# Attention scores of two heads in one alternating block, with the gate's matmul on 64 rows

## The reference

```python
log_f = jax.nn.log_sigmoid((proj[..., 3 * D:] + b_f).astype(jnp.float32))
cum = jnp.cumsum(log_f, axis=1).transpose(0, 2, 1)
s = jnp.einsum('bqhd,bkhd->bhqk', q, k) * HEAD_DIM ** -0.5
s = s + cum[:, :, :, None] - cum[:, :, None, :]
s = jnp.where(mask, s, -jnp.inf)
pr = jax.nn.softmax(s, axis=-1)
out = jnp.einsum('bhqk,bkhd->bqhd', pr, v)
```

## Time and profile before

| | |
|---|---|
| Time, median of 3 runs | 1496.22 us (1495.9 to 1497.05) |
| Span of the profiled execution | 1498.1 us (its own time outside the span is not shown) |
| TensorE busy | 1415.4 us, 94% of the span |
| TensorE weight loads | 1242.7 us, 83% |
| VectorE busy | 1002.6 us, 67% |
| ScalarE busy | 807.3 us, 54% |
| GpSimd busy | 423.5 us, 28% |
| Granted TensorE clock, mean | 0.972 of full speed |
| First score matmul of layers 0, 1, 2, 3 | 91.99, 470.9, 813.52, 1185.3 us |

### The profile page before, as it was taken

How to read it: one execution, slowest core, us unless ns; L and a number is a source line. 1 busy time by engine, 2 the same in 40 slices (tenths; PEclk the granted TensorE clock), 3 DMA queues, 4 the chain that set the end, 5 groups by cost and what they waited for, 6 DMA issues and landing times. The chain is left out here.

```text
span 1498.1 us, 24861 instructions
## 1 busy us (share of the span) xinstructions
PE 1415.4 (94%) x8532; PEld 1242.7 (83%) x8532; DVE 1002.6 (67%) x1577; ACT 807.3 (54%) x1397; POOL 423.5 (28%) x459
## 2 busy tenths in 40 slices
PE   5989899999998989999987989999999899999998
PEld 4767799988776779998876879998878677999986
DVE  4757677764766867775566867776476665777644
ACT  4536466653544746664354656665355454666533
POOL 3521023320165603331027102332006311233200
PEclk9989999999999999999998799999999899999999
DMA  7422265564553345566452136566454322555651
GB/s 281 158 89 82 99 203 178 187 199 145 187 195 129 113 140 173 178 184 198 165 186 88 43 106 191 181 184 197 153 189 155 126 71 85 184 181 184 197 180 57
DMA packets 63927, 232.99 MB, mean 156 GB/s; under 512 B 7184, under 2 KB 7312, under 8 KB 63856
## 3 DMA queue, kind: packets, MB, share of 16 engines
q1 hardware_dynamic: 61056, 221.87, 45.1%
q0 software_dynamic: 2800, 10.18, 2.2%
HBM read 230.97 MB, written 1.05 MB: 155 GB/s over the span
## 5 line engine op out<-in xcount | busy, mean ns | idle before, releaser
L607 DVE TENSOR_TENSOR w_lo<-w_raw,w_hi 128x1024 fp32r<-128x1024 f32 x418 | 561.8, 1383 | 123.2 <-ACT w_hi L379 122.4
L379 ACT ACTIVATE w_hi<-w_raw 128x1024 fp32r<-128x1024 f32 x418 | 420.0, 1052 | 152.7 <-PE bank L1073 112.3
L1049 PE MATMUL bank<-hT_hi,w_hi 128*128 128x256 f32 x1408 | 400.9, 285 | 4.3 <-DVE hT_lo L661 4.3
L1050 PE MATMUL bank<-hT_lo,w_hi 128*128 128x256 f32 x1408 | 400.4, 284 | 0.0
L1051 PE MATMUL bank<-hT_hi,w_lo 128*128 128x256 f32 x1408 | 400.4, 284 | 0.0
L1049 PEld LDWEIGHTS bank<-hT_hi,w_hi 128*128 128x128 f32 x1408 | 271.2, 193 | 5.1 <-issue 5.1
L1050 PEld LDWEIGHTS bank<-hT_lo,w_hi 128*128 128x128 f32 x1408 | 271.3, 193 | 0.0
L1051 PEld LDWEIGHTS bank<-hT_hi,w_lo 128*128 128x128 f32 x1408 | 271.1, 193 | 0.0
L1035 POOL TENSOR_TENSOR gate_c<-gate_c,up_c 128x256 f32<-128x256 f32 x88 | 105.2, 1195 | 293.1 <-ACT gate_c L582 293.1
L887 DVE SCALAR_TENSOR_TENSOR gate_c<-bank,conv_sb,gate_c 128x255 f32<-128x255 f32 (+1 forms) x176 | 84.1, 478 | 120.5 <-ACT up_c L578 120.5
L1049 PE MATMUL bank<-w_hi,hT_hi 128*128 128x512 f32 (+1 forms) x336 | 136.0, 405 | 12.5 <-DVE w_lo L607 6.8
(11 more groups left out here) (136 smaller groups left out, 2289.8 us busy)
## 6 DMA issues: line engine op xcount, KB each, us to landing
w_raw<-weights SPq DMA_DIRECT2D x418, 512.0 KB, 3.9
gain<-gains POOLq DMA_DIRECT2D x11, 512.0 KB, 4.8
rel<-rel_in POOLq DMA_DIRECT2D x4, 512.0 KB, 6.4
x<-x_in SPq DMA_DIRECT2D x2, 512.0 KB, 6.2
p_raw<-p_in POOLq DMA_DIRECT2D x4, 256.0 KB, 5.1
out<-x SPq DMA_DIRECT2D x2, 512.0 KB, 2.6
gain<-gains SPq DMA_DIRECT2D x1, 512.0 KB, 6.4
consts<-consts_in POOLq DMA_DIRECT2D x1, 488.0 KB, 6.3
```

Source lines behind the costliest of these rows:

```text
L379: nc.scalar.activation(w_hi[:, slot, q * HALF:(q + 1) * HALF], w_raw[:, raw, :], ACT.Copy).then_inc(hi_ready, 1)
L607: nc.vector.tensor_tensor(w_lo[:, slot, cols], w_raw[:, half(q)[0], :], w_hi[:, slot, cols].bitcast(F32), ALU.subtract).then_inc(lo_ready, 1)
L1049: nc.tensor.matmul(out_ap, l_hi, r_hi, start=start, stop=False, skip_group_check=True)
L1050: nc.tensor.matmul(out_ap, l_hi, r_lo, start=False, stop=False, skip_group_check=True)
```

## The change

`scores(h)` becomes `score_pair(pair)`. Its matmuls alternate between the two heads of the pair: high x high of the even head (rows 0 to 63), high x high of the odd one (rows 64 to 127), then high x low of both, low x high of both. In FoX the gate's matmul uses the 64 rows of its head's half in place of all 128; for that `cum` and `sel` get a second copy, from row 64 on, by one more ScalarE and one more VectorE instruction in each FoX layer, and by constants. `score_pair(0)` stands ahead of the loop, and the others in odd steps: in step h, the scores of heads h + 1 and h + 2, which wait for the masks of heads up to h.

```diff
                         act.wait_ge(cum_zero, 1)
+                        nc.scalar.activation(cum[HD:HD + HEADS, :], fz[:], ACT.Copy)
                         nc.scalar.activation(cum[0:HEADS, :], fz[:], ACT.Copy).then_inc(cum_hi_ready, 1)
...
                         dve.wait_ge(cum_hi_ready, k + 1)
-                        nc.vector.tensor_tensor(cum[CUM_LO:CUM_LO + HEADS, :], fz[:], cum[0:HEADS, :].bitcast(F32),
-                                                ALU.subtract).then_inc(cum_ready, 1)
+                        for r in (HD + CUM_LO, CUM_LO):
+                            ins = nc.vector.tensor_tensor(cum[r:r + HEADS, :], fz[:], cum[0:HEADS, :].bitcast(F32), ALU.subtract)
+                        ins.then_inc(cum_ready, 1)
...
-                def scores(h):
-
-                    g = HEADS * L + h
-                    if h >= 2:
-                        pe.wait_ge(s_min, 2 * (g - 1))
-                    if m == SWA and h == 8:
+                def score_pair(pair):
+
+                    g = HEADS * L + 2 * pair
+                    if pair:
+                        pe.wait_ge(s_min, 2 * g)
+                    if m == SWA and pair == 4:
                         pe.wait_ge(qkT_ready, item0 + 6)
-                    r = slice((h % 2) * HD, (h % 2) * HD + HD)
-                    kp = h // 8 if m == SWA else h // 2
+                    kp = pair // 4 if m == SWA else pair
+                    halves = [slice(0, HD), slice(HD, P)]
                     for qb in range(2):
-                        dst = aux[h % 2][:, qb * SEQ:(qb + 1) * SEQ]
+                        cols = slice(qb * SEQ, (qb + 1) * SEQ)
                         ts = slice(qb * P, (qb + 1) * P)
-                        last = three(dst, qT_hi[r, h // 2, ts], qT_lo[r, h // 2, ts], kT_hi[r, kp, :], kT_lo[r, kp, :],
-                                     True, m != FOX)
+                        for left, right in ((qT_hi, kT_hi), (qT_hi, kT_lo), (qT_lo, kT_hi)):
+                            for e, r in enumerate(halves):
+                                last = nc.tensor.matmul(aux[e][:, cols], left[r, pair, ts], right[r, kp, :],
+                                                        start=left is qT_hi and right is kT_hi,
+                                                        stop=m != FOX and left is qT_lo, skip_group_check=True)
+                                if qb == 1 and m != FOX and left is qT_lo:
+                                    last.then_inc(s_done, 1)
                         if m == FOX:
-                            last = nc.tensor.matmul(dst, sel[:, h:h + 1].to_broadcast([P, P]), cum[:, :],
-                                                    start=False, stop=True, skip_group_check=True)
-                    last.then_inc(s_done, 1)
+                            for e, r in enumerate(halves):
+                                h = 2 * pair + e
+                                last = nc.tensor.matmul(aux[e][:, cols], sel[r, h:h + 1].to_broadcast([HD, P]), cum[r, :],
+                                                        start=False, stop=True, skip_group_check=True)
+                                if qb == 1:
+                                    last.then_inc(s_done, 1)
...
-                scores(0)
+                score_pair(0)
                 for h in range(HEADS + LAG):
                     if 2 <= h < HEADS + 2:
                         transpose_p(h - 2)
-                    if h + 1 < HEADS:
-                        scores(h + 1)
+                    if h % 2 and h + 1 < HEADS:
+                        score_pair((h + 1) // 2)
                     if h >= LAG:
                         values(h - LAG)
...
-    c[:HEADS, C_SEL:C_COS] = c[CUM_LO:CUM_LO + HEADS, C_SEL:C_COS] = np.eye(HEADS)
+    for r in (0, CUM_LO, HD, HD + CUM_LO):
+        c[r:r + HEADS, C_SEL:C_COS] = np.eye(HEADS)
```

## The result

| | before | after |
|---|---|---|
| Time, median of 8 runs each | 1497.8 us | 1510.2 us |
| Ratio of the times | | 1.0075 (95% interval 1.0054 to 1.0096), some 11 us slower |
| Profiled execution: time, span | span 1498.1 us | 1512.0 us, 1510.2 us |
| TensorE busy | 1415.4 us | 1385.4 us |
| Mean granted clock | 0.972 | 0.957 |

The account below looks back on a forecast made before the run. TensorE was taken to set FoX's pace, with a closed loop through VectorE's mask added. FoX twice 6.3 us in all, relative-position 6.4 and sliding-window 9.6 summed to +22: time 1518 us, range 1490 to 1528.

Parts of the forecast that it names:

- the likeliest case's own range: Whole kernel: the range of the forecast with spacing 0.12 us, 1512 to 1524 us, chance 0.42.
- the prediction's own sign: Neighbouring 64-row matmuls of different halves: a start-to-start time near 0.06 us would show the forecast wrong, 0.12 right.
- Spacing p: Pair's score block: time between successive 64-row matmuls, taken as 0.12 us, making a FoX pair's scores 2.10 us.
- The wait: Loop bodies: TensorE waits for VectorE's fresher mask; 4.11 us plus scores, 6.21 a pair in FoX against 5.52 before.
- rival (3): Sliding-window or relative-position loop: half clock adds about 3 us for each of four or more pairs; 1530 to 1545, chance 0.08.
- rival (1): Score blocks: halves overlap fully, p = 0.06; relative-position layer loses 2 us, sliding-window 5, FoX gains; 1496, chance 0.30.
- (2): Score blocks: the halves overlap in part, p about 0.09, half the sum; 1507 us, chance 0.10.
- The start: Loop starts: fourth pair waits for head 5's mask, +1.7 us FoX, +2.3 relative-position; sliding-window start +5; FoX clock gains 0.8.
- The layers: Sums by layer: FoX +3.2 us each, relative-position +6.4, sliding-window +9.6.
- What a loop loses is lost: After the loops: TensorE is fed as before, so nothing lost in a loop comes back; no size given.
- The gate: FoX scores: 128-row gate matmul costs leaving and re-entering 64-row form per query block, 0.54 us where three spacings are 0.36.

Follow-up runs that it names:

- number 3: The change with the two heads of a pair one after the other instead of alternating; 1528.9 us, ratio 1.0197.
- a fill of 5: The change with 5 needless 128-row matmuls ahead of each pair's scores from step 5 on; 1491.9 us, ratio 0.9964.
- number 2: The kernel before with only the gate's matmul put on 64 rows, single heads and old waits kept; 1481.5 us, ratio 0.9886.
- number 1: The change with the values of head h - 3 issued ahead of the pair's scores in odd steps; 1483.7 us, ratio 0.9888.
- 4: The change with 12 needless 128-row matmuls ahead of each pair's scores from step 5 on; 1495.8 us, ratio 0.9974.

## Why the prediction was right in its outcome and wrong in its terms

The sign, the range and the wait's place were right: slower, 1510 in 1490 to 1528, with TensorE waiting for the mask ahead of each pair. The forecast's sum of +22 was nearly twice too high (+12.4 by the medians), the time lies below the likeliest case's own range (1512 to 1524), and by the prediction's own sign, a spacing near 0.06, its case was wrong. That 1510 is nearer to the forecast's 1518 than to the 1496 of the right spacing is luck: two misses of opposite sign.

- **Spacing p (the step that failed).** Taken as 0.12, on the ground that a load's 0.107 us for one half would queue behind the other's; measured 0.06, and a block of 1.14 us where the sum had 2.10. The loads of the two halves run at the same time, x2 in 0.19 us. The rows before could not show it, as no two halves stood side by side. The rule of the Trainium skill (TensorE: Matmul & The Clock Gate, Part 3) that matmuls on different row groups run concurrently is borne out by this trace: the two records of a couple together are as long as one (0.28 us). Without alternation (number 3) the kernel is 1.2% slower than the change, 19 us.
- **The wait.** Predicted as a closed loop of 4.11 us plus the block. Measured in FoX at full clock 5.27 from block to block (121.90 to 127.17), and 5.36 a pair with a fill of 5 (transposes 118.48 to 145.39, less two units): the sum with p = 0.06 gave 5.37, with a block of 1.26. The block was 1.14, as the halves start in couples and one spacing of 0.12 fewer is paid; 4.11 + 1.14 is 5.25. In the relative-position layer it was 5.26 (499.90 to 505.16), with a block of 0.91: 0.24 more than 4.11 + 0.91, a term that the sum lacked. VectorE's mask waited 0.28 us there for `rel`, which GpSimd writes. There were 22 waits for the mask, in all 40.8 us, where the trace before had 0.4. From number 2 to number 3, pairing with little overlap and with the fresher wait, the ratio goes from 0.9886 to 1.0197: 3.1%, some 47 us, its half-clock time included. What number 1 shows is that this is a matter of where the block stands, not of pairing.
- **The clock.** It was rival (3), with 3 us for each of four or more pairs, to be added to the forecast's own p; it came about with rival (1)'s p instead. Rival (1) alone would have been 1496, and the fill of 5, which leaves the loop as long as it was, shows the size of what the clock added: some 17 to 18 us for 46 us less at half clock. The two misses, 0.06 too much of p and a clock left as it was, had opposite signs. The range was made to reach over rivals (1) and (2) and left (3) out, so what came, (1)'s spacing with (3)'s clock, lies in it because the two cancel, and the chance of 0.08 for the clock was too low.
- **The start.** The clock did return sooner in the FoX loop (0.82 against 0.50 in the window 95 to 100), as taken at 0.8 us. The fourth pair waited 3.4 us for the mask of head 5, the longest wait of the list. Its scores began 4.89 us after the transposes of head 2 (110.98 to 115.87), where the earlier trace rows gave 4.84.
- **The layers.** The forecast had +3.2 us for each FoX layer, 6.4 for the relative-position and 9.6 for the sliding-window layer. FoX came out at 1.6 less and 0.6 more (1.0 more ahead of the first loop). The sliding-window layer lost 5.3 us, as rival (1)'s 5; the relative-position layer 6.8, where rival (1) had 2: the clock there was 0.97 before and 0.85 after, and that it did most of this is likely but not shown for the layer alone.
- **After the loops.** "What a loop loses is lost" was right to a few us only: the shifted MLP start of layer 0 met a half-clock stretch that it had not before. Why it does so there and not in numbers 1, 2 and 4 stays open; it was not tried by itself.
- **The gate.** Its edges were known and priced inside the pair, but that this one edit alone is worth 1.1% was seen only by number 2.

The parts as steps from one measured kernel to the next: gate's edit 0.9886, pairing with the fresher wait 1.0315 (number 2 to 3), alternation 0.988 (number 3 to the change). They multiply to 1.0075 by their making, and taken in another order each could have another size.

## What to carry to other kernels

A block that is issued earlier or in larger pieces on an in-order engine needs its operands' buffers earlier too: write down the closed loop through the engines that free them, and put independent work of the same engine ahead of the waiting instruction. Two edits in one change are to be priced one by one, since here the small one gained 17 us and the large one lost more. And here TensorE's idle time cost twice: the wait itself, and slower matmuls behind it, so a time saved on TensorE that turns into waiting in every pair can make a kernel slower.

## What the runs showed of the hardware that was not expected

- Two 64-row matmuls on rows 0 to 63 and 64 to 127, into different banks, run fully at the same time, their weight loads too: a couple every 0.12 us at full clock and every 0.21 at half clock. If issued one half after the other, they overlap only at the seam, in number 3 four and four of eight matmuls, or three and three of six.
- 100 needless matmuls in TensorE's waits made the kernel 18 us faster (1510.2 to 1491.9), with the half-clock time going from about 118 to 72 us. In the change the clock fell in the score blocks behind waits of 1.77 us (those that start at 127.17 and 136.70), though not behind every such wait (behind the one that ends at 514.51 it stayed at 1.00 to 517).
- In the kernel before, in FoX, a 64-row matmul follows the 128-row gate after 0.32 us and the next one after 0.22 (121.22, 121.54, 121.76), where neighbours of one form have 0.12; a 128-row matmul follows a 64-row one after 0.20. At half clock the same distances are 0.51, 0.38 and 0.34, where neighbours have 0.21. The second matmul behind the transposes is late too when it is a 128-row one (0.20, 124.11 to 124.31 in the kernel after), so not all of the 0.22 belongs to the 64-row form.
